# Gate and up weights of the experts loaded as halves of four chunks

## The reference

```python
g_idx = jnp.argmax(g_logits, axis=-1)                 # the best of 8 groups of experts
top_val, top_idx = lax.top_k(e_logits, TOP_K)         # the best 2 of the 8 experts in it
h = jax.nn.silu(xb @ w_gate[e]) * (xb @ w_up[e])      # 1024 -> 512
return h @ w_down[e]                                  # 512 -> 1024
```

## Time and profile before

| what | value |
|---|---|
| median of 3 runs | 1372.3 us |
| the profiled execution | 1382.97 us |
| its span | 1381.2 us |
| PE (matmul) busy | 1042.7 us, 75% |
| PE weight loads busy | 676.5 us, 49% |
| VectorE busy | 456.4 us, 33% |
| ScalarE busy | 298.1 us, 22% |
| packets of the SyncE queue | 70400, 461.00 MB, 81.7% of 16 DMA engines' span |
| read from memory, over the span | 462.59 MB, 336 GB/s with the writes |

### The profile page before, as it was taken

How to read it: one execution, slowest core, us unless ns; L and a number is a source line. 1 busy time by engine, 2 the same in 40 slices (tenths; PEclk the granted TensorE clock), 3 DMA queues, 4 the chain that set the end, 5 groups by cost and what they waited for, 6 DMA issues and landing times.

```text
span 1381.2 us, 21752 instructions
## 1 busy us (share of the span) xinstructions
PE 1042.7 (75%) x9279; PEld 676.5 (49%) x9279; DVE 456.4 (33%) x1008; ACT 298.1 (22%) x627; POOL 36.1 (3%) x34
## 2 busy tenths in 40 slices
PE   8998999999999987565756757666565756657565
PEld 6997788878776544232423323233232423324232
DVE  4687785787943421110111111011110111111112
ACT  4654352644631211010110100010010110100000
POOL 0000101011101000000000000000000000000000
PEclk9999999999987999897888888888897888988898
DMA  9462444405573799999999999999999999999996
GB/s 323 147 237 71 145 173 155 141 33 207 185 316 145 253 424 427 426 425 426 428 424 427 426 425 428 427 424 427 428 425 427 427 425 428 428 424 427 426 424 263
DMA packets 71237, 464.35 MB, mean 336 GB/s; under 512 B 6874, under 2 KB 15892, under 8 KB 38548
## 3 DMA queue, kind: packets, MB, share of 16 engines
q1 hardware_dynamic: 70400, 461.00, 81.7%
q10 hardware_dynamic: 788, 2.66, 0.5%
HBM read 462.59 MB, written 1.05 MB: 336 GB/s over the span
## 4 chain that ended last, share of the span: by engine, by line
DMA 48%; PE 42%; DVE 6%; ACT 1%; SPq 1%; issue 1%; POOL 0%; DVEq 0%; ACTq 0%
DMA ring<-in_w_up 45%; PE bank L1918 15%; PE bank L2382 13%; PE bank L1875 3%; DMA spare<-in_w_up 3%; PE bank L1987 2%; PE bank L1899 2%; PE bank L1960 2%; DVE ring_lo L1199 1%; SPq L587 1%; PE bank L2402 1%; PE bank L2013 1%; DVE qk L1158 1%; DVE ring_lo L1204 1%; PE bank L1934 0%
## 5 line engine op out<-in xcount | busy, mean ns | idle before, releaser
L2382 PE MATMUL bank<-ring,expert_area 128*32 128x256 f32 x3840 | 312.5, 492 | 216.5 <-DMA ring<-in_w_up 216.5
L2382 PEld LDWEIGHTS bank<-ring,expert_area 128*32 128x32 f32 x3840 | 144.4, 136 | 377.3 <-DMA ring<-in_w_up 236.5
L1918 PE MATMUL bank<-ring_lo,xt_hi 128*128 128x512 f32 (+3 forms) x576 | 182.9, 386 | 1.3 <-ACT wide L846 0.8
L1762 DVE TENSOR_TENSOR expert_area<-expert_area,bank 128x128 f32<-128x128 f32 x64 | 18.3, 286 | 461.2 <-ACT expert_area L1089 461.2
L1089 ACT ACTIVATE expert_area<-bank 128x128 f32<-128x128 f32 x64 | 17.8, 278 | 610.6 <-PE bank L2382 610.6
L2402 PE MATMUL bank<-ring,consts 128*32 128x256 f32 x1952 | 118.0, 382 | 26.9 <-DVE consts L1764 26.9
L1918 PEld LDWEIGHTS bank<-ring_lo,xt_hi 128*128 128x128 f32 x576 | 104.0, 188 | 21.2 <-issue 4.4
L2402 PEld LDWEIGHTS bank<-ring,consts 128*32 128x32 f32 x1952 | 60.1, 109 | 67.0 <-DVE consts L1764 20.1
L1918 PE MATMUL bank<-ring_lo,xt_lo 128*128 128x512 f32 (+2 forms) x240 | 91.1, 380 | 0.0
L1768 DVE COPY consts<-bank 32x256 f32<-32x256 f32 x63 | 26.5, 421 | 130.8 <-PE bank L2402 130.7
L2471 PE MATMUL bank<-consts,expert_area 128*128 128x512 f32 x120 | 55.1, 601 | 16.2 <-DVE consts L1769 16.2
(11 more groups left out here) (314 smaller groups left out, 1247.6 us busy)
## 6 DMA issues: line engine op xcount, KB each, us to landing
ring<-in_w_down SPq DMA_DIRECT2D x60, 2048.0 KB, 24.9
ring<-in_w_gate SPq DMA_DIRECT2D x59, 2048.0 KB, 18.4
ring<-in_w_up SPq DMA_DIRECT2D x58, 2048.0 KB, 22.9
ring<-in_moba_w_kv SPq DMA_DIRECT2D x4, 2048.0 KB, 8.2
ring<-in_moba_w_in SPq DMA_DIRECT2D x4, 2048.0 KB, 8.0
ring<-in_w_in SPq DMA_DIRECT2D x3, 2048.0 KB, 8.3
ring<-in_mla_w_uq SPq DMA_DIRECT2D x4, 1152.0 KB, 5.9
ring<-in_mla_w_o SPq DMA_DIRECT2D x2, 2048.0 KB, 8.0
```

Of the source, the lines that this page charges most:

```text
L1918: last = nc.tensor.matmul(dst, x[at], w[:, c, :], start=(piece == 0 and c == 0 and w is hi and x is x_hi), stop=(piece == 1 and c == per - ...
L2382: last = nc.tensor.matmul(hidden_in[SLOTS * j:SLOTS * j + SLOTS, :], picked[:, c, SLOTS * i:SLOTS * i + SLOTS], both[:, :, c, j // 2, j % ...
```

## The change

`load_expert` issues four transfers of 1 MiB where it issued two of 2 MiB: the first four chunks of w_gate, the first four of w_up, the last four of w_gate, the last four of w_up. The first two raise a new semaphore, `first_half_landed[parity]`, the last two `gate_up_landed[parity]`, each by 32 in sum. TensorE waits for the first, does the 32 matmuls of the chunks 0 to 3, waits for the second and does the other 32. The number of matmuls, their order and their shapes stay; w_down and the experts 0 to 7 and 63 stay as they were.

```diff
             def load_expert(e, parity, gate_up_free, down_free):
                 gate_up_free()
-                for k, name in enumerate(("w_gate_2", "w_up_2")):
-                    gate_or_up(name, e, ring[:, 3 * parity + k, :], gate_up_landed[parity])
+                for half in range(2):
+                    at = slice(2048 * half, 2048 * half + 2048)
+                    for k, name in enumerate(("w_gate_2", "w_up_2")):
+                        src = t[name][0, bass.ds(e, 1)].rearrange("e (p c) f -> p (e c f)", c=KD)
+                        sp.dma_start(ring[:, 3 * parity + k, at], src[:, at]).then_inc(
+                            (gate_up_landed if half else first_half_landed)[parity], 16)
                 down_free()
                 down(e, ring[:, 5 - 3 * parity, :], down_landed[parity])
...
-                else:
-                    pe.wait_ge(gate_up_landed[i % 2], 64 * (n - 2) + (32 * (i // 2) + 32 - 32 * unsignalled * (i % 2)))
+                count = None if fixed is not None else 64 * (n - 2) + (32 * (i // 2) + 32 - 32 * unsignalled * (i % 2))
+                for half in range(2):
+                    if count is not None:
+                        pe.wait_ge((gate_up_landed if half else first_half_landed)[i % 2], count)
+                    if i == 0:
+                        pe.wait_ge(picked_ready, 2 * n + half + 1)
+                    gate_and_up(i, gate_up, range(4 * half, 4 * half + 4), fixed == 0 and i == 0)
                 if i == 0:
-                    for half in range(2):
-                        pe.wait_ge(picked_ready, 2 * n + half + 1)
-                        gate_and_up(i, gate_up, range(4 * half, 4 * half + 4), fixed == 0)
                     turn_weights(n)
-                else:
-                    gate_and_up(i, gate_up, range(KD))
                 transpose_hidden(x)
```

More of the change, by code:

```diff
@@ L416, in build @@
         gate_up_landed = [sem(f"gate_up_landed{i}") for i in range(2)]
+        first_half_landed = [sem(f"first_half_landed{i}") for i in range(2)]
         down_landed = [sem(f"down_landed{i}") for i in range(2)]
```

## The result

The changed kernel takes 1379.05 us, a median of 5 runs (1378.23 to 1381.77), beside 1371.44 us (1370.62 to 1372.55) for the kernel before: a ratio of 1.0051 with a 95% interval of 1.0029 to 1.0073, so 7.0 us slower (4.0 to 10.0); the two medians lie 7.6 us apart. Forecast were 6.0 us, and 1378.3 us for the time.

The account below looks back on a forecast made before the run. The stream of weights was taken to bound the expert stage: 6.4 us for more packets less 0.4 us at the end gives 6.0 us, 1372.3 + 6.0 = 1378.3 us; range of 8 in 10: 1374.5 to 1381.0 us.

Parts of the forecast that it names:

- The bound: Expert stage: the stream of weights bounds it at 426 GB/s, so slots freed earlier gain 0 us in 55 experts.
- The price of the packets: Gate and up transfers in 55 experts: 16 more packets per expert and engine at 9.7 ns each, 8.5 us slower.
- The overlap correction: Expert stream: packets on an engine overlap by 4.2 ns each, which lowers the price from 13.9 to 9.7 ns.
- the second rival: Expert stream: overlap does not grow with packets, or alternating pieces disturb reads, and end clock drops: 1381 to 1387 us; chance 0.07.
- The other end: Lower figure for the packets' price, from the last landings of expert 63's halves: 0.04 us per expert, 2.2 us.
- From the profiled execution to the runs: Recording may cause part of the profile's extra 10.7 us; the middle of 4.3 and 8.5 us was taken, 6.4 us.
- the span of about 1389 us: Whole profiled execution of the changed kernel: growth of 8.5 - 0.4 = 8.1 us, nothing taken off for recording.
- The end: Last expert: earlier products let TensorE end 0.97 us behind the last landing, 0.45 us gained.
- The sum: Whole kernel: 6.4 us for packets less 0.4 us at the end, 6.0 us slower, 1378.3 us.
- The new wait: Expert stage: a new short wait of TensorE's w_down products (L2402) for w_down must appear.
- the longer way from issue to landing of the last halves: Expert stage: issue to landing longer by 2 to 3 us for the last halves.
- The loss from a cold clock at the end: Last matmuls: if new short waits drop the clock they take up to twice as long, 2.5 us lost; not taken.

Follow-up runs that it names:

- e6: Kernel before, but SyncE waits for the w_down slot before it issues gate and up: 1372.27 us, ratio 0.9994.
- e5: Kernel before, profiled once more without an edit: median 1372.12 us, ratio 0.9999; its profiled execution took 1371.72 us.
- e1: Changed kernel, but TensorE waits for both halves before its first product: 1380.57 us, ratio 1.0078 to the kernel before.

## Why the prediction was right, and where it was not

**The bound.** Right: the stream of weights sets the expert stage, with DMA engines at 1.01 in both windows from 484 to 1340 us, and the slots freed earlier bought nothing in it. e6 shows it from the other side.

**The price of the packets.** 9.7 ns per packet and 8.5 us were worked out from the earlier trace rows; eight kernels give 9.0 to 9.6 ns, and the changed one 0.152 us per expert, 8.4 us. The overlap correction was needed: without it the sum would have been 12.2. That the overlap grows with the packets, which the second rival doubted, can be read from the changed kernel: its 30901 packets take 1.013 x 16 x 600 = 9725 us, 0.3147 each, and 48 of them 15.11 us in a period of 14.91, so each overlaps by 4.1 ns as before. The other end, 2.2 us from the last landings, was far off: it took 2.467 us for each MiB in 8 KB packets, where the stream has 14.911 / 6 = 2.485, and the small difference of two large terms took up the error. The prediction's own reason against it, that most of the engines had finished by then, may be the cause; no run was made for it. The Trainium skill's 3 cycles per packet (DMA: Bandwidth & Descriptors, Why small descriptors are slow), 3.5 ns as an estimate, are a third of what is measured; the measurement decides.

**From the profiled execution to the runs.** Wrong: the prediction took the middle between all and nothing of the 10.7 us for the recording, which took 2.1 us off the 8.5. e5 shows that they belong to the dense stage, so the term is nothing. For the same reason the span of about 1389 us that was forecast for the profiled execution came out as 1376.4. The row that would have told it stood in the page of the kernel before, the granted clock in tenths by slice; e5's follows it:

```profile
PEclk9999999999987999897888888888897888988898
```
```profile
PEclk9999999999999999788988979889888988988898
```

The 8 and the 7 in the 12th and 13th slice lie ahead of the expert stage, where e5 has 9 throughout.

**The end.** A small gain was forecast, 0.45 us; these traces don't fix its size. TensorE at the end of e5 and of the changed kernel:

```profile
1337.76 6.41 PE L2382 MATMUL bank<-ring,expert_area 128*32 128x256 f32 x64 [6.12 <-DMA ring<-in_w_up]
1344.90 0.33 PE L2394 MATMUL bank<-consts,expert_area 128*128 128x128 f32 x1 [0.73 <-DVE expert_area L1762]
1345.61 1.93 PE L2402 MATMUL bank<-ring,consts 128*32 128x256 f32 x32 [0.38 <-DVE consts L1764]
1348.62 3.67 PE L2492 MATMUL bank<-consts,expert_area 96*128 96x512 f32 x8 [1.08 <-DVE consts L1769]
1352.22 3.85 PE L2382 MATMUL bank<-ring,expert_area 128*32 128x256 f32 x64
1356.78 0.33 PE L2394 MATMUL bank<-consts,expert_area 128*128 128x128 f32 x1 [0.71 <-DVE expert_area L1762]
1357.49 1.93 PE L2402 MATMUL bank<-ring,consts 128*32 128x256 f32 x32 [0.38 <-DVE consts L1764]
```
```profile
1340.42 2.03 PE L2387 MATMUL bank<-ring,expert_area 128*32 128x256 f32 x32 [1.43 <-DMA ring<-in_w_up]
1345.49 3.61 PE L2387 MATMUL bank<-ring,expert_area 128*32 128x256 f32 x32 [3.05 <-DMA ring<-in_w_up]
1349.83 0.33 PE L2399 MATMUL bank<-consts,expert_area 128*128 128x128 f32 x1 [0.73 <-DVE expert_area L1767]
1350.54 1.93 PE L2407 MATMUL bank<-ring,consts 128*32 128x256 f32 x32 [0.38 <-DVE consts L1769]
1353.55 3.67 PE L2497 MATMUL bank<-consts,expert_area 96*128 96x512 f32 x8 [1.08 <-DVE consts L1774]
1357.71 2.02 PE L2387 MATMUL bank<-ring,expert_area 128*32 128x256 f32 x32 [0.48 <-DMA ring<-in_w_up]
1360.19 2.02 PE L2387 MATMUL bank<-ring,expert_area 128*32 128x256 f32 x32 [0.47 <-DMA ring<-in_w_up]
...
1363.64 1.07 PE L2407 MATMUL bank<-ring,consts 128*32 128x256 f32 x16 [0.38 <-DVE consts L1769]
1365.11 1.07 PE L2407 MATMUL bank<-ring,consts 128*32 128x256 f32 x16 [0.39 <-DMA ring<-in_w_down]
```

In e5 nothing after 1337.76 us waits for a transfer: the last lands at about 1357.4 us and the products end at 1359.42, 2.0 us behind. In the changed kernel they wait four more times and end 1.2 us behind the last landing. That is 0.9 us, but two other traces keep it from being the price of the early products. The same kernel's distance was 1.4 us in the profile of before. And e1, in which nothing begins early, also comes to wait for the last half of w_down and ends 1.2 us behind:

```profile
1366.39 1.07 PE L2407 MATMUL bank<-ring,consts 128*32 128x256 f32 x16 [0.38 <-DVE consts L1769]
1367.80 1.07 PE L2407 MATMUL bank<-ring,consts 128*32 128x256 f32 x16 [0.34 <-DMA ring<-in_w_down]
```

So the end gives from nothing to 0.9 us, and the forecast 0.45 lies within. From the first expert product to the last landing e5 takes 896.4 us and the changed kernel 904.2: 7.9 more, for 8.4 by the period.

**The sum.** 8.4 from the packets less up to 0.9 at the end is 7.5 to 8.4, within the measured 4.0 to 10.0. The forecast 6.0 lies 1 us under the measured 7.0, the same sum without the wrong term, 8.1, lies 1 us over it: the time can't tell the two apart, and it is e5 that does. That 6.0 stands so near is in this part luck.

**The new wait** for w_down came as forecast. So did the longer way from issue to landing of the last halves: as medians of the experts loaded from 700 to 1300 us, the last half of w_up takes 24.9 us where the whole took 22.9, that of w_gate 21.6 for 18.4. The 22.3 and 19.0 of the DMA view above mix first and last halves. w_down took 26.7 for 24.9. The loss from a cold clock at the end did not come: the granted clock was 1.00 from 1357.7 to 1366.2 us.

## What to carry to other kernels

When a stage is bound by its transfers (DMA share at 1, rate flat), starting the work on them earlier can only gain at the stage's end, while in this kernel smaller packets were paid for in every one: count packets, not transfers, and look for the tensor that could still move in longer rows. A tail that looks like a chain of matmuls may be just ahead of the stream; its slack is the distance between the last landing and the last product. And check that the profiled execution is a typical one, stage by stage, before a difference to the median is put on anything.

## What was not expected of the hardware

- With gate and up each in one transfer into partitions 0 to 63 and one into 64 to 127, the stream (w_down included) ran at half the rate (215 GB/s for 426); with one into the even and one into the odd partitions at the full rate.
- 64 products of 256 moving columns in 32-bit take 3.83 us at a stride of two elements and 7.43 us at a stride of four, both at full clock. The Trainium skill (SBUF — State Buffer, The DMA port swizzle) has lines of 16 bytes, each of which should be hit at least twice; at a stride of four 4-byte elements it is hit once, and the trace agrees with that. The same note gives four 32-bit elements as the stride that is free, and there the 7.43 us are against it; the measurement decides.
- A packet costs 9.0 to 9.6 ns beside its bytes even at 4, 8 and 16 KB: 1.5% of the period (14.911 us for 14.686) between gate, up and down all in 8 KB and all in 16 KB.
